# Rotary embedding in a fused two-block kernel: 32-row exchanges by transfer in place of rotation matmuls

## The reference

```
ckr    = rms_norm(x, norm_kv) @ w_dkv            # 256 latent + 64 rope columns
k_rope = apply_rope(ckr[..., 256:], cos, sin)    # one rope key for all heads
k_nope = c_kv @ w_uk;  v = c_kv @ w_uv
u      = rms_norm(x, norm_b) @ w_in              # 384 query latent + 1024 gate
q      = rms_norm(u[..., :384]) @ w_uq           # per head 128 nope + 64 rope
q_rope = apply_rope(q[..., 128:], cos, sin)
out    = softmax(mask(q_nope k_nope' + q_rope k_rope') * scale) @ v
y      = (out * silu(gate)) @ w_out

def apply_rope(x, cos, sin):
    x1, x2 = split(x)                            # two halves of 32
    return concat([x1 * cos - x2 * sin, x2 * cos + x1 * sin])
```

## Time and profile before

| | |
|---|---|
| time, three runs | 2555.8, 2559.78, 2561.72 us (median 2559.78) |
| span of the profiled execution | 2559.3 us; its own time is not listed apart from the three |
| TensorE | 2500.2 us busy (98%), 13018 matmuls, mean granted clock 0.994 |
| VectorE / ScalarE / GpSimd | 63% / 39% / 42% busy |
| DMA | 199 MB, mean 78 GB/s |

### The profile page before, as it was taken

One profiled execution on the slowest core, in us unless ns is written; L12 is line 12 of the kernel. 1 busy time (PEld: TensorE's weight loads), 2 busy tenths in 40 slices (PEclk: granted clock), 3 DMA queues, 4 the chain that ended last, 5 costly groups with the idle time before them and its releaser, 6 DMA issues.

```text
span 2559.3 us, 33797 instructions
## 1 busy us (share of the span) xinstructions
PE 2500.2 (98%) x13018; PEld 2073.5 (81%) x13018; DVE 1614.0 (63%) x1965; ACT 990.8 (39%) x1405; POOL 1069.6 (42%) x776
## 2 busy tenths in 40 slices
PE   8999999999999899999999999999999999999998
PEld 6878888887788778888878878788888787889986
DVE  5685723476554677677688785678774533556555
ACT  5254245322322443333354453355641421444432
POOL 3464523211233478888861113333355332111134
PEclk9999999999999999999999999999999999999999
DMA  3111121111441022222287522211132311000033
GB/s 136 50 34 34 46 76 44 63 46 38 155 154 50 33 91 77 91 80 83 91 208 187 144 62 82 96 48 41 41 123 82 117 59 38 20 20 18 25 108 123
DMA packets 62724, 199.39 MB, mean 78 GB/s; under 512 B 6528, under 2 KB 13952, under 8 KB 61184
## 3 DMA queue, kind: packets, MB, share of 16 engines
q1 hardware_dynamic: 49472, 150.75, 17.6%
q10 hardware_dynamic: 6208, 35.27, 3.6%
q0 software_dynamic: 6912, 11.54, 2.8%
HBM read 159.27 MB, written 32.51 MB: 75 GB/s over the span
## 4 chain that ended last, share of the span: by engine, by line
PE 82%; DVE 11%; ACT 4%; issue 2%; POOL 1%; DMA 0%; ACTq 0%; SPq 0%; DVEq 0%; POOLq 0%
PE ps L1006 8%; PE ps L1008 8%; PE ps L1007 8%; PE ps L1079 5%; PE ps L1081 5%; PE ps L1080 5%; PE ps L1340 5%; PE ps L1339 5%; PE ps L1341 5%; PE ps L1371 2%; PE ps L1373 2%; PE ps L1372 2%; PE ps L1541 2%; PE ps L1259 1%; PE ps L1276 1%
## 5 line engine op out<-in xcount | busy, mean ns | idle before, releaser
L741 POOL TENSOR_TENSOR derived_vectors<-w_staged 1x1 f32<-1x1 f32 x146 | 37.1, 254 | 1183.1 <-PE ps L1008 481.0
L746 POOL TENSOR_TENSOR w_low<-w_staged,w_high 128x1024 fp32r<-128x1024 f32 x146 | 393.0, 2692 | 11.4
L1079 PE MATMUL ps<-h_mix_high,w_high 128*128 128x512 f32 x688 | 279.5, 406 | 0.0
L1081 PE MATMUL ps<-h_mix_high,w_low 128*128 128x512 f32 x688 | 269.6, 392 | 0.0
L1080 PE MATMUL ps<-h_mix_low,w_high 128*128 128x512 f32 x688 | 269.3, 391 | 0.0
L1081 PEld LDWEIGHTS ps<-h_mix_high,w_low 128*128 128x128 f32 x688 | 129.7, 189 | 28.0
L1079 PEld LDWEIGHTS ps<-h_mix_high,w_high 128*128 128x128 f32 x688 | 130.2, 189 | 26.3 <-issue 0.5
L1080 PEld LDWEIGHTS ps<-h_mix_low,w_high 128*128 128x128 f32 x688 | 130.1, 189 | 25.6 <-issue 0.5
L742 POOL CAST w_high<-w_staged 128x1024 fp32r<-128x1024 f32 x146 | 150.2, 1029 | 0.0
L2711 DVE TENSOR_TENSOR squares<-ps,squares 128x512 f32<-128x512 f32 x88 | 60.5, 688 | 108.5 <-PE ps L1341 107.8
L1006 PE MATMUL ps<-h_rnn_high,w_high 128*128 128x512 f32 x320 | 125.0, 391 | 1.6 <-DVE h_rnn_low L2284 1.6
(11 more groups left out here) (556 smaller groups left out, 7111.9 us busy)
## 6 DMA issues: line engine op xcount, KB each, us to landing
w_staged<-weights_in SPq DMA_DIRECT2D x168, 512.0 KB, 3.6
w_staged_late<-weights_in SPq DMA_DIRECT2D x22, 512.0 KB, 4.4
gates_loaded<-gates ACTq DMA_DIRECT2D x8, 1024.0 KB, 7.4
gates<-tmp SPq DMA_DIRECT2D x16, 512.0 KB, 2.6
act_raw<-gates SPq DMA_DIRECT2D x16, 512.0 KB, 7.7
gates<-gates_staged_late SPq DMA_DIRECT2D x22, 256.0 KB, 2.0
x_in<-xT_in SPq DMA_DIRECT2D x8, 512.0 KB, 8.3
x_mid<-xT_in ACTq DMA_DIRECT2D x1, 4096.0 KB, 15.2
```

What stands on the lines that cost most here:

```text
L746: nc.gpsimd.tensor_tensor(w_low[:, j], w_staged[:, j], f32(w_high[:, j]), ALU.subtract).then_inc(s_split, 1)
L1079: nc.tensor.matmul(ps[:, bank], wH, h1H[:, c, tok], start=(c == 0), stop=False)
L1081: done = nc.tensor.matmul(ps[:, bank], wL, h1H[:, c, tok], start=False, stop=(c == DC - 1))
```

## The change

- The matrix `rotate`, its load, and all matmuls with it are gone: two for the key, two for each pair of heads.
- Key: behind `dkv`, ScalarE's queue sends four transfers of 32 rows x 1024 from `tmp` to `k_rope` with the halves exchanged. ScalarE turns the sign of the sine table for rows 0 to 31 and 64 to 95, after the table has landed. VectorE makes sine product, cosine product and sum before its first read of a gate tile.
- Queries: SyncE's queue sends four transfers of 32 rows x 512 for each half of tokens from `q_rope` to `rotated`, behind the load of the next pair's first unit. VectorE's three instructions for a half stand on their own (`mla_rope_turned`): for pair 0 between piece 5 and piece 6, for the other pairs at the end of steps 2 and 3 of the odd head.
- Pieces are numbered 0 to 13; the fillers are shifted so that each step keeps the projections that it had.

```diff
+        def exchanged_rows():
+            return [(slice(64 * b + 32 * k, 64 * b + 32 * k + 32), slice(64 * b + 32 * (1 - k), 64 * b + 32 * (1 - k) + 32))
+                    for b in range(2) for k in range(2)]
...
+            def exchange_query_halves(p):
+                for h in range(2):
+                    sp.wait_ge(s_pread, PIECES * p + h + 1)
+                    for out, source in exchanged_rows():
+                        sp.dma_start(rotated[out, half_of(h)], q_rope[source, half_of(h)]).then_inc(s_rotq[h], 16)
...
             def load_mla_pair(p):
...
                 load_columns(u, K_UNIT + 4 + 3 * g, 3, 2 * P, k * P, P, None, s_load[u % 2])
+                if p:
+                    exchange_query_halves(p - 1)
...
-            pe.wait_ge(s_cconst, 48)
             pe.wait_ge(s_ldone, 4)
-            for h in range(2):
-                nc.tensor.matmul(ps[:, 6 + h], rotate[:], tmp[:, half_of(h)], start=True, stop=True).then_inc(s_rot, 1)
...
-                elif i in (3, 5):
-                    h = i // 2 - 1
-                    pe.wait_ge(s_pread, 16 * p + h + 1)
-                    nc.tensor.matmul(ps[:, bank], rotate[:], q_rope[:, half_of(h)], start=True, stop=True).then_inc(s_rotq, 1)
...
-                    act.dma_start(rotate[:], a["rotate"]).then_inc(s_cconst, 16)
+                    for out, source in exchanged_rows():
+                        act.dma_start(k_rope[out], tmp[source]).then_inc(s_rot, 16)
...
             act.wait_ge(s_cwl, 5)
-            act.wait_ge(s_cconst, 32)
+            act.wait_ge(s_cconst, 16)
             act.dma_start(cos_sin[:], a["cos_sin"]).then_inc(s_cconst, 16)
             nc.scalar.activation(causal_r[:], causal[:], ACT.Copy).then_inc(s_ldone, 1)
+            act.wait_ge(s_cconst, 32)
+            for rows in (slice(0, 32), slice(64, 96)):
+                nc.scalar.activation(cos_sin[rows, 1], cos_sin[rows, 1], ACT.Copy, scale=-1.0).then_inc(s_ldone, 1)
...
+            dve.wait_ge(s_rot, 64)
+            dve.wait_ge(s_ldone, 6)
+            nc.vector.tensor_tensor(k_rope[:], k_rope[:], cos_sin[:, 1], ALU.mult).then_inc(s_kr, 1)
+            nc.vector.tensor_tensor(tmp[:], tmp[:], cos_sin[:, 0], ALU.mult).then_inc(s_kr, 1)
+            dve.wait_ge(s_kr, 2)
+            nc.vector.tensor_tensor(k_rope[:], k_rope[:], tmp[:], ALU.add).then_inc(s_kr, 1)
             dve.wait_ge(s_xs5, 16)
             scaled("cgate", cgate)
-            for h in range(2):
-                dve.wait_ge(s_rot, h + 1)
-                nc.vector.tensor_tensor(sq[:, 0, half_of(h)], ps[:, 6 + h], cos_sin[:, 1, half_of(h)], ALU.mult).then_inc(s_kr, 1)
-            nc.vector.tensor_tensor(k_rope[:], tmp[:], cos_sin[:, 0], ALU.mult).then_inc(s_kr, 1)
-            dve.wait_ge(s_kr, 3)
-            nc.vector.tensor_tensor(k_rope[:], k_rope[:], sq[:, 0], ALU.add).then_inc(s_kr, 1)
             dve.wait_ge(s_krH, 1)
...
+            def mla_rope_turned(p, h):
+                x, turned = q_rope[:, half_of(h)], rotated[:, half_of(h)]
+                dve.wait_ge(s_rotq[h], 64 * (p + 1))
+                nc.vector.tensor_tensor(turned, turned, cos_sin[:, 1, half_of(h)], ALU.mult).then_inc(s_rqe, 1)
+                nc.vector.tensor_tensor(x, x, cos_sin[:, 0, half_of(h)], ALU.mult).then_inc(s_rqe, 1)
+                dve.wait_ge(s_rqe, 4 * p + 2 * h + 2)
+                nc.vector.tensor_tensor(x, x, turned, ALU.add).then_inc(s_qready, 1)
...
-            for m in range(12):
+            for m in range(10):
                 if m == 6:
+                    for h in range(2):
+                        mla_rope_turned(0, h)
                     mla_rope_low(0)
                 mla_read(m)
...
+                if H % 2 and H < 7 and r in (2, 3):
+                    mla_rope_turned(H // 2 + 1, r - 2)
```

More of the change, by code:

```diff
@@ L65 @@
 LOADS = _u
-MLA_COUNT = {0: 8, 1: 16, 2: 20, 4: 24, 6: 26, 7: 28, 8: 30, 9: 32, 10: 34, 11: 36, 12: 40, 13: 44, 14: 46, 15: 48}
-MLA_FILLERS = {0: ((), (12,), (13,), (14,), (15,), (), (), ()), 1: ((16,), (17, 18), (19, 20), (21, 22), (23,), (24,), (25, 26), (27,))}
+PIECES = 14
+MLA_COUNT = (8, 16, 20, 24, 26, 28, 30, 32, 34, 36, 40, 44, 46, 48)
+MLA_FILLERS = {0: ((), (10,), (11,), (12,), (13,), (), (), ()), 1: ((14,), (15, 16), (17,), (18,), (19,), (20,), (21, 22), (23,))}
 def mla_fillers(n):
     H, r = n // 8, n % 8
-    return [16 * (H // 2) + i for i in MLA_FILLERS[H % 2][r]] if H < 7 else []
+    return [PIECES * (H // 2) + i for i in MLA_FILLERS[H % 2][r]] if H < 7 else []
 K_UNIT = STAGE["uqr0"][0]
@@ L429, in fused_kernel @@
         s_c2, s_cs, s_crstd, s_cw, s_cwh, s_cwl = [sem(f"latent_{n}") for n in ("square", "sum", "rstd", "chain", "high", "low")]
-        s_rot, s_kr, s_cg = sem("k_rotated"), sem("k_rope_chain"), sem("mla_gate_silu")
-        s_rotq, s_rqe, s_qready = [sem(f"q_rope_{n}") for n in ("rotated", "chain", "ready")]
+        s_rot, s_kr, s_cg = sem("k_halves_exchanged"), sem("k_rope_chain"), sem("mla_gate_silu")
+        s_rqe, s_qready = [sem(f"q_rope_{n}") for n in ("chain", "ready")]
+        s_rotq = [sem(f"q_rope_half{h}_exchanged") for h in range(2)]
         s_pread, s_normed = sem("mla_projection_read"), sem("mla_probs_normed")
@@ L723, in _ @@
                 load_mla_pair(p)
+            exchange_query_halves(3)
             items_of(sp, K_UNIT + 20, lambda i, j: load(i, j, 2), K_UNIT + 12)
@@ L973, in mla_bank @@
         def mla_bank(m):
-            return m % 4 if m < 12 else 7
+            return m % 4 if m < 10 else 7
         def mla_done(m):
-            return MM_PER_UNIT * (K_UNIT + 3 * (m // 16)) + MLA_COUNT[m % 16]
+            return MM_PER_UNIT * (K_UNIT + 3 * (m // PIECES)) + MLA_COUNT[m % PIECES]
         Y_PARTS = [(m, slice(0, S)) for m in (0, 2, 4, 6)] + [(m, half_of(h)) for h in (1, 0) for m in (1, 3, 5, 7)]
@@ L1464, in mla_projection @@
             def mla_projection(m):
-                p, i = m // 16, m % 16
+                p, i = m // PIECES, m % PIECES
                 u0, bank = K_UNIT + 3 * p, mla_bank(m)
@@ L2169, in _ @@
             items_of(act, DC, mla_gate)
-            act.wait_ge(s_kr, 4)
+            act.wait_ge(s_kr, 3)
             nc.scalar.activation(k_ropeH[:, 0], k_rope[:], ACT.Copy).then_inc(s_krH, 1)
             def mla_high(m):
[L2175 to L2180, removed]
+                p, i = m // PIECES, m % PIECES
+                t, h = i // 10, i % 2
+                if i in (2, 3, 10, 11):
+                    dst = q_nopeH
+                elif i in (4, 5, 12, 13):
+                    dst = k_nopeH
                 else:
@@ L3060, in mla_read @@
             def mla_read(m):
-                p, i = m // 16, m % 16
-                t, bank = i // 12, ps[:, mla_bank(m)]
+                p, i = m // PIECES, m % PIECES
+                t, h, bank = i // 10, i % 2, ps[:, mla_bank(m)]
                 if i in (0, 1):
@@ L3066, in mla_read @@
                     nc.vector.tensor_copy(q_rope[:, half_of(i)], bank).then_inc(s_pread, 1)
[L3067 to L3070, removed]
-                    nc.vector.tensor_tensor(turned, bank, cos_sin[:, 1, half_of(h)], ALU.mult).then_inc(s_pread, 1)
-                    nc.vector.tensor_tensor(x, x, cos_sin[:, 0, half_of(h)], ALU.mult).then_inc(s_rqe, 1)
-                    dve.wait_ge(s_rqe, 2 * p + h + 1)
-                    dve.wait_ge(s_pread, m + 1)
-                    nc.vector.tensor_tensor(x, x, turned, ALU.add).then_inc(s_qready, 1)
-                elif i in (2, 4, 12, 13, 6, 7, 14, 15):
-                    h = {2: 0, 4: 1, 12: 0, 13: 1, 6: 0, 7: 1, 14: 0, 15: 1}[i]
-                    H, L = (q_nopeH, q_nopeL) if i in (2, 4, 12, 13) else (k_nopeH, k_nopeL)
-                    dve.wait_ge(s_qnH, 8 * p + {2: 1, 4: 2, 6: 3, 7: 4, 12: 5, 13: 6, 14: 7, 15: 8}[i])
+                elif i in (2, 3, 10, 11, 4, 5, 12, 13):
+                    H, L = (q_nopeH, q_nopeL) if i in (2, 3, 10, 11) else (k_nopeH, k_nopeL)
+                    dve.wait_ge(s_qnH, 8 * p + {2: 1, 3: 2, 4: 3, 5: 4, 10: 5, 11: 6, 12: 7, 13: 8}[i])
                     low_of(L[:, t, half_of(h)], bank, H[:, t, half_of(h)]).then_inc(s_pread, 1)
                 else:
-                    r = 2 * (i - 8)
+                    r = 2 * (i - 6)
                     dve.wait_ge(s_mm, mla_done(m))
```

22 lines of the change are left out of this document (10 added, 12 removed).

## The result

The changed kernel is slower. Its four runs have a median of 2570.08 us (2568.91 to 2571.64), four runs of the kernel before on the same chip 2559.53 (2555.8 to 2561.72): a ratio of 1.0048, 95% interval 1.0036 to 1.0060. (The ratio is recorded with its interval and is not the quotient of the two medians, which is 1.0041.) The forecast was 2567.7, in a range of 2560 to 2575. The profiled run took 2568.91 us, with a span of 2567.1.

A forecast was written before the change was run, and what follows sets the result against it. TensorE, busy for 98% of the span, was taken as the bound. Terms 10.6 + 2.6 - 0.9 + 0.5 - 4.9 = +7.9 us on the 2559.3 span gave 2567.2, plus 0.5 for the median: 2567.7, range 2560 to 2575.

The forecast's parts named there:

- Gate stop: Before the first gate read: table load, sign and three key instructions hold VectorE, so TensorE waits, +10.6 us.
- Clock behind it: After TensorE's wait at the gate: its granted clock falls to half for a while, +2.6 us, ends 0 and 3.4.
- Pair 0: Ahead of the first scores: VectorE finishes later than TensorE, leaving -0.9 us of 4.8 saved; clock shifts there net +0.5.
- The exchanges: SyncE's query transfers within SBUF: they land before VectorE asks, in pair 0 and later pairs, costing nothing.
- Fillers: Attention of pairs 1 to 3: six query rotation passes of 0.86 us leave the chain, 0.3 given back, -4.9 us.
- dearer hand-over: Rival: key instructions run contended (+3.8) or pair 0's exchange lands late (+3.5); some 12 us in all, 2571.6; chance 0.14.
- wash: Rival: TensorE stops at the gate, but without clock loss, and scores start when TensorE is ready; +0.6, 2560.4; chance 0.16.
- faster rival: Rival: key rotation hides behind the gate tiles, first gate read before 2088.7, only saved passes count; -5.3, 2554.5; chance 0.08.

The follow-up runs named there:

- no_turn: Changed kernel with the three VectorE turning instructions per query half of pairs 1 to 3 replaced by a one-column copy, transfers kept: 2564.52 us, ratio 1.0030 to before.
- host_sign: Changed kernel with the sign already in the sine table as loaded and ScalarE's two sign instructions removed: 2568.61 us, ratio 1.0051 to the kernel before.
- q_mid: Changed kernel with the turned halves of pairs 1 to 3 placed between row maximum and filler read: 2563.76 us, ratio 1.0027 to the kernel before.
- key_mid: Changed kernel with the key's three VectorE instructions placed behind the reads of the third gate tile: 2557.51 us, ratio 1.0001 to the kernel before.
- key_end: Changed kernel with the key's three VectorE instructions placed behind all gate reads: 2563.31 us, ratio 1.0024 to the kernel before.
- best: Changed kernel with key instructions behind the third gate tile, turned halves before the filler read, and VectorE's pair 0 order changed: 2546.93 us, ratio 0.9964 to before.

## Why the prediction was right, and which step failed

- **Gate stop, +10.6: measured +10.61.** Its parts are rows now. From the end of the low parts (2079.59) to the sign's start 4.76 us for issue and landing, 2.13 for the sign (2.0 taken), then 3.53 from the first key instruction to the gate read (3.7), uncontended as argued: GpSimd had nothing to do in the stop.
- **Clock behind it, +2.6: measured +1.46** in the profiled run, and 1.68, 2.44 and 2.70 in no_turn, host_sign and q_mid, whose stops were of 9.3 to 11.3 us. The middle of the range was fair and the ends of 0 and 3.4 held; the single run has a spread of a good microsecond.
- **Pair 0, -0.9 and +0.5: measured -1.26** for both. VectorE was the later one, as worked out: from the last gate read to the start of the first scores it takes 1.12 us less than before (21.50 against 22.62), with a wait of 4.4 us (4.7 forecast). The half clock moved into the first scores (+1.45 up to the row maximum of head 0) and left its old place (-1.59 from there to head 1), so the net of the clock was -0.1, where +0.5 was forecast.
- **The exchanges, 0.** The issues took 0.59 us in the median (0.56 forecast), the landing 2.0 (1.8). The exchange's lines in the view of the tile, kernel after: issues with their count, least, median and most ns, first and last start; then us to landing:

```profile
L619 SPq DMA_DIRECT2D q_rope_rotated<-q_rope x32: 507/590/768, 2163.4 to 2378.1; - x32
...
DMA to landing us min/median/max: 1.9/2.0/2.3
```

Neither VectorE nor TensorE has a wait for them, in pair 0 or later, and none for SyncE's later loads.
- **Fillers, -4.9, ends -5.2 and -3: measured +0.86. This is the step that failed.** What the prediction let be given back, 0.3, was 6.06, 2.0 for each pair. The passes did leave TensorE's path: q_mid shows the full -5.20. The failed part is the price of the move of VectorE's three instructions. The step noted that the copy of the transposes would come later, and worked out its 0.3 from no row. Each turned half is 2.0 us of VectorE work; put ahead of the copy and the next maximum, it holds what follows these on ScalarE and TensorE, and the second one also holds ScalarE's high part of the queries. Rows for a better price were in the kernel before: VectorE reached the copy with 0.36 us to spare, against 2.0 us of work that was to come ahead of it, while 1.35 us ahead of the read of the filler were idle even with that work in front.
- **Why the total was near all the same.** With the fillers at +0.9 instead of -4.9 the sum is 5.8 us higher, and the clock and pair 0 are 2.0 lower (1.1 and 0.9): +7.9 + 5.8 - 2.0 = +11.7. So the sum was too low by half of itself, and the range, wide for the sake of other terms, took it in: that the place on VectorE would cost 5.8 us was no part of it. The median of the runs is 2.4 above the forecast. The profiled run is the fastest of the four, 1.2 below their median, and its time is 1.8 above its span, where the forecast had added 0.5; in the profile itself the lead of 3.9 us made up for the error of 3.8.
- **The rivals.** The dearer hand-over (2571.6) lies nearer to the median measured than the forecast does, but by neither of its mechanisms: the key instructions took 1.22 each and no exchange came late. Its contention is real in another place, in key_mid and key_end. The wash needed a clock without loss and scores that start when TensorE is ready; neither happened. The faster rival had its condition, a first gate read within 5.3 us of the old one, and that was missed by as much again. Where the condition is met (key_mid) the time is the same as before, not faster, since the fillers had been given back; with both mended it is -5.9 us, near the -5.3 that the rival had named.

## What to carry to other kernels

An instruction on an engine with a fixed order is priced by what is queued behind it: place it in an idle gap of that engine, behind what its consumers already wait for, and look up who waits for the next ones. Matmuls that are taken off the critical path pay only if the instructions that replace or move with them are placed as carefully; here the same operations in other places were worth 10.6 us of stop, the clock behind it, and 2.0 us a pair. To weigh such terms, compare stages from a common start inside each profile, not whole spans: the untouched part alone moved by up to 5.3 us between profiles (2074.72 to 2079.97).

## What the runs showed of the hardware

- **VectorE beside GpSimd.** A key instruction of 1024 columns with both inputs in SBUF took 1.22 us alone and 1.64 to 3.41 beside a GpSimd split, which itself took 3.24 or 3.25 where it has 2.40 undisturbed. The Trainium skill (SBUF — State Buffer, "SBUF: two separate sides") says that such a pair exclude each other for a whole instruction and the other fully blocks. The trace agrees, and in both directions. In key_mid, VectorE's first starts while GpSimd's cast runs to 2094.68; with 1.22 behind that it would end at 2095.90, and does at 2095.76. GpSimd's split, waiting for it, would end 2.40 later, at 2098.16, and does at 2098.01. VectorE's second, waiting for the split, would end at 2099.23, and does at 2099.09. Each comes out to 0.15 us. The same sum gives the ends of all three VectorE instructions of key_end and of the low part behind them, each to 0.15 us.
- **Rows cost ScalarE nothing here.** Two instructions of 32 rows x 1024 took 2.13 us together; 128 x 1024 took 1.06 each.
- **A transfer within SBUF** of 32 rows x 512 (64 KB) landed 1.9 to 2.3 us after its issue. Each issue held SyncE 0.51 to 0.77 us, about as long as one of its unit loads (0.56 in the median). On ScalarE's queue the key's four of 32 rows x 1024 took 0.61 each and landed after 2.4, where the issue of the table's load took 0.33.
- **The clock behind a stop is not the same twice.** Stops of 11.2 and 11.3 us in the same place cost 1.46, 1.68 and 2.70 us behind them. The wait of 1.9 us ahead of the first transposes had a granted clock of 0.57 behind it in the kernel before and in best, and of 1.00 in the kernel after (2188 to 2192), where it follows the longer stop. Why was not tried.
